# Sliding-window attention in two layers: the two key blocks of a query block folded into 128 columns

## What is computed

```python
WINDOW = BLOCK = 128
kb, vb = band(k), band(v)      # the previous block of 128 keys and the own one: 256 keys
s = einsum('bnqkgd,bnskd->bnkgqs', qb, kb) * HEAD_DIM ** -0.5
rel = qi + BLOCK - sj          # qi: query in its block, sj: key in the band
mask = (rel >= 0) & (rel < WINDOW) & (kpos >= 0)
s = where(mask, s, -inf)
m = maximum(max(s), sink)
p = exp(s - m)
p = p / (sum(p) + exp(sink - m))
o = einsum('bnkgqs,bnskd->bnqkgd', p, vb)
```

## Time and profile before

| | |
|---|---|
| median of 3 runs | 2209.37 us (2207.12 to 2209.56) |
| the profiled execution | 2209.6 us |
| its span, first to last instruction | 2207.7 us |
| TensorE busy | 2189.7 us (99%) |
| VectorE busy | 1191.6 us (54%) |
| ScalarE busy | 977.1 us (44%) |
| GpSimd busy | 1059.2 us (48%) |
| attention groups of layer 0 | about 129.8 to 279 us of the span |
| attention groups of layer 1 | 675.9 us later, the same pattern |

### The profile page before, as it was taken

The page is one execution under the profiler, slowest core; times in us unless marked ns, Lnnn a source line. Parts: engine busy times, 40 slices in busy tenths (PEclk is TensorE's granted clock), DMA queues, the critical chain, the costliest instruction groups (busy, mean ns, idle before and its releaser), DMA issues.

```text
span 2207.7 us, 29108 instructions
## 1 busy us (share of the span) xinstructions
PE 2189.7 (99%) x10471; PEld 1763.7 (80%) x10473; DVE 1191.6 (54%) x1536; ACT 977.1 (44%) x1549; POOL 1059.2 (48%) x525
## 2 busy tenths in 40 slices
PE   9999999999999999999999999999999999999999
PEld 7877778888888887778888888887787678888887
DVE  7877863222446877874222345858787745333301
ACT  5567633322214567744333214336645654444311
POOL 4963344444444883244444443433666653444442
PEclk9999999999999999999999999999999999999999
DMA  5332232333662332132333572321221012333332
GB/s 179 107 89 58 67 96 86 98 99 98 209 210 88 110 100 61 58 88 94 95 95 95 179 239 87 96 82 63 69 93 49 29 55 87 101 99 96 95 95 86
DMA packets 62870, 219.58 MB, mean 99 GB/s; under 512 B 7936, under 2 KB 8192, under 8 KB 62784
## 3 DMA queue, kind: packets, MB, share of 16 engines
q1 hardware_dynamic: 55296, 191.16, 29.0%
q10 hardware_dynamic: 7488, 27.27, 3.6%
HBM read 212.76 MB, written 2.10 MB: 97 GB/s over the span
## 4 chain that ended last, share of the span: by engine, by line
PE 92%; DVE 4%; ACT 2%; issue 1%; POOL 1%; DMA 0%; SPq 0%; ACTq 0%; POOLq 0%; DVEq 0%
PE bank L1691 28%; PE bank L1693 27%; PE bank L1692 27%; PE bank L1874 1%; PE bank L1946 1%; PE bank L1920 1%; PE bank L1765 1%; PE bank L2229 1%; ACT prob L650 1%; PE bank L2240 1%; POOL soft_lo L473 0%; DVE conv L1260 0%; PE bank L2273 0%; DVE conv L1262 0%; DMA raw<-stream 0%
## 5 line engine op out<-in xcount | busy, mean ns | idle before, releaser
L390 POOL TENSOR_TENSOR wl<-raw,wh 128x1024 fp32r<-128x1024 f32 x349 | 852.6, 2444 | 1029.9 <-ACT wh L529 1029.8
L1691 PE MATMUL bank<-hh,wh 128*128 128x512 f32 (+1 forms) x1984 | 775.2, 391 | 5.4 <-ACT root L866 2.1
L1693 PE MATMUL bank<-hh,wl 128*128 128x512 f32 (+1 forms) x1984 | 765.1, 386 | 0.0
L1692 PE MATMUL bank<-hl,wh 128*128 128x512 f32 (+1 forms) x1984 | 764.5, 385 | 0.0
L529 ACT ACTIVATE wh<-raw 128x1024 fp32r<-128x1024 f32 x351 | 369.7, 1054 | 586.5 <-PE bank L1693 543.9
L1691 PEld LDWEIGHTS bank<-hh,wh 128*128 128x128 f32 x1984 | 373.4, 188 | 90.4 <-issue 11.1
L1693 PEld LDWEIGHTS bank<-hh,wl 128*128 128x128 f32 x1984 | 373.4, 188 | 75.7
L1692 PEld LDWEIGHTS bank<-hl,wh 128*128 128x128 f32 x1984 | 373.7, 188 | 74.5 <-issue 1.7
L1691 PE MATMUL bank<-ah,wh 128*128 (+1 forms) x512 | 201.7, 394 | 0.0
L1693 PE MATMUL bank<-ah,wl 128*128 (+1 forms) x512 | 200.7, 392 | 0.0
L1692 PE MATMUL bank<-al,wh 128*128 (+1 forms) x512 | 198.7, 388 | 0.0
(11 more groups left out here) (374 smaller groups left out, 2786.0 us busy)
## 6 DMA issues: line engine op xcount, KB each, us to landing
raw<-stream SPq DMA_DIRECT2D x351, 512.0 KB, 3.6
ada_w<-ada ACTq DMA_DIRECT2D x48, 512.0 KB, 4.5
x<-x_t ACTq DMA_DIRECT2D x4, 512.0 KB, 7.7
out_t<-x SPq DMA_DIRECT2D x8, 256.0 KB, 2.1
th<-q SPq DMA_DIRECT2D x16, 64.0 KB
th<-q SPq DMA_DIRECT2D x64, 16.0 KB
q<-th SPq DMA_DIRECT2D x16, 64.0 KB, 2.0
cst<-consts SPq DMA_DIRECT2D x1, 640.0 KB, 5.7
```

The costliest lines, as they stand in the source:

```text
L390: nc.gpsimd.tensor_tensor(wl[:, slot, :], raw[:, raw_slot, :], wh[:, slot, :].bitcast(F32), ALU.subtract).then_inc(lo_ready, 1)
L1691: mm(dst, wh[:, slot, w], xh, start=start, stop=False)
L1692: mm(dst, wh[:, slot, w], xl, start=False, stop=False)
L1693: return mm(dst, wl[:, slot, w], xh, start=False, stop=stop)
```

## The change

Scores of a query block are no longer accumulated on a mask. TensorE writes both key blocks' scores to PSUM as they are. ScalarE copies the previous block's 128 columns (or, for n = 0, the mask) to `prob` in SBUF (`base`), VectorE overwrites those columns that belong to the own block (`copy_predicated`, with the constant `later`), and maximum, exponentials and normalisation then work on 128 columns in SBUF. TensorE makes four transposes for every group. ScalarE copies the transposed weights out once; VectorE multiplies them by the constant `keep`, which leaves those of the own block (`keep_own`). The value product uses the identity: all weights times V of the previous block, plus kept weights times (V own - V previous), the difference being made once a layer (`v_step`, in the memory of `v_t`). `prob_t` and the PSUM bank of the transposes become double. The mask matmuls, `put_mask` and the semaphore `masked` go; `base_ready` and `kept_out` are new. The diff, with unchanged lines and semaphore declarations cut:

```diff
--- before.py
+++ after.py
@@ -100,8 +100,8 @@
...
-            prob = sb("prob", [P, 2, 4, 2 * P], F32, region)
-            prob_t = sb("prob_t", [P, 2, 4, P], F32, region)
+            prob = sb("prob", [P, 2, 4, P], F32, region)
+            prob_t = sb("prob_t", [P, 2, 2, 4, P], F32, region)
...
@@ -313,6 +313,16 @@
...
+        def kept_before(l, g):
+            return 12 * l + g - (g + 3) // 4
+        def score_block(g, w):
+            b = 2 * (g % 2)
+            return bank[:, b:b + 2, :].rearrange("p a (c w d) -> p (a c) w d", c=2, w=2)[:, :, w, :]
+        turned_bank = lambda g: 5 - g % 2
+        v_step = v_t[:, :].rearrange("p (a b) -> p a b", a=BLK)
...
@@ -640,24 +650,20 @@
...
                 def exps(g):
...
-                    lo = P if n == 0 else 0
-                    b = 2 * (g % 2)
...
-                    if g >= 2:
-                        act.wait_ge(turned, 16 * l + g - 1)
...
-                        kv, at = i // 2, n * NH + 2 * (2 * j + i % 2) + i // 2
-                        af(prob[:, g % 2, i, lo:], bank[:, b + kv, (i % 2) * 2 * P + lo:(i % 2 + 1) * 2 * P], ACT.Exp,
+                        at = n * NH + 2 * (2 * j + i % 2) + i // 2
+                        af(prob[:, g % 2, i, :], prob[:, g % 2, i, :], ACT.Exp,
...
-                def put_mask(g):
-                    lo = P if group(g)[0] == 0 else 0
-                    b = 2 * (g % 2)
-                    act.wait_ge(exp_ready, 16 * l + g - 1)
-                    af(bank[:, b:b + 2, :].rearrange("p a (c d) -> p (a c) d", c=2)[:, :, lo:],
-                       win_mask[:, lo:2 * P].unsqueeze(1).to_broadcast([P, 4, 2 * P - lo]), ACT.Copy).then_inc(masked, 1)
+                def base(g):
+                    act.wait_ge(scores_ready, 16 * l + g + 1)
+                    if g >= 2:
+                        act.wait_ge(turned, 16 * l + g - 1)
+                    before = score_block(g, 0) if group(g)[0] else win_mask[:, P:2 * P].unsqueeze(1).to_broadcast([P, 4, P])
+                    af(prob[:, g % 2, :, :], before, ACT.Copy).then_inc(base_ready, 1)
...
@@ -667,17 +673,16 @@
...
+                base(0)
+                base(1)
                 exps(0)
...
-                put_mask(2)
...
                 def probs_out(g):
...
-                    if g >= 1:
-                        act.wait_ge(pv_ready, 16 * l + g)
-                    if group(g)[0] > 0:
-                        af(prob_t[:, 0, :, :], bank[:, 4, :].rearrange("p (a b) -> p a b", a=4), ACT.Copy)
-                    af(prob_t[:, 1, :, :], bank[:, 5, :].rearrange("p (a b) -> p a b", a=4), ACT.Copy).then_inc(turned_out, 1)
+                    if g >= 2:
+                        act.wait_ge(pv_ready, 16 * l + g - 1)
+                    af(prob_t[:, g % 2, 0, :, :], bank[:, turned_bank(g), :].rearrange("p (a b) -> p a b", a=4), ACT.Copy).then_inc(turned_out, 1)
...
@@ -687,17 +692,16 @@
...
                 for g in range(CO_FROM):
                     probs_out(g)
+                    if g + AHEAD < 16:
+                        base(g + AHEAD)
...
-                        put_mask(3)
...
                         exps(g + AHEAD)
-                    if g + 2 * AHEAD < 16:
-                        put_mask(g + 2 * AHEAD)
...
                     if g == LN_MEAN:
@@ -716,6 +720,7 @@
...
                 probs_out(13)
+                base(15)
                 exps(15)
...
@@ -1145,7 +1150,9 @@
...
                 dve.wait_ge(vt_turned, l + 1)
-                nc.vector.tensor_copy(v[:, :, :], bank[:, M_VT % 4, :].rearrange("p (a b) -> p a b", a=BLK)).then_inc(lin_free, 2)
+                v_bank = bank[:, M_VT % 4, :].rearrange("p (a b) -> p a b", a=BLK)
+                link(nc.vector.tensor_copy(v[:, :, :], v_bank))
+                tt(v_step[:, 1:BLK, :], v_bank[:, 1:BLK, :], v[:, 0:BLK - 1, :], ALU.subtract).then_inc(lin_free, 2)
                 invert(q_scale[:, :], q_root[:, :])
...
@@ -1153,11 +1160,13 @@
...
                 def maxima(g):
...
-                    lo, b, s = (P if n == 0 else 0), 2 * (g % 2), g % 2
+                    s = g % 2
...
-                    link(nc.vector.reduce_max(row_max[:, s, :], bank[:, b:b + 2, :].rearrange("p a (c d) -> p (a c) d", c=2)[:, :, lo:], AX.X))
+                    dve.wait_ge(base_ready, 16 * l + g + 1)
+                    link(nc.vector.copy_predicated(prob[:, s, :, :], minus_later.bitcast(I32).unsqueeze(1).to_broadcast([P, 4, P]), score_block(g, 1)))
+                    link(nc.vector.reduce_max(row_max[:, s, :], prob[:, s, :, :], AX.X))
...
@@ -1165,13 +1174,20 @@
...
                 def normalise(g):
-                    (n, j), s = group(g), g % 2
-                    lo = P if n == 0 else 0
+                    s = g % 2
...
-                    w = 2 * P - lo
-                    tt(prob[:, s, :, lo:], prob[:, s, :, lo:], rden[:, s, :].unsqueeze(2).to_broadcast([P, 4, w]), ALU.mult).then_inc(probs_ready, 1)
+                    tt(prob[:, s, :, :], prob[:, s, :, :], rden[:, s, :].unsqueeze(2).to_broadcast([P, 4, P]), ALU.mult).then_inc(probs_ready, 1)
+                def keep_own(g):
+                    if group(g)[0] == 0:
+                        return
+                    dve.wait_ge(turned_out, 16 * l + g + 1)
+                    if g >= 2:
+                        dve.wait_ge(pv_ready, 16 * l + g - 1)
+                    tt(prob_t[:, g % 2, 1, :, :], bank[:, turned_bank(g), :].rearrange("p (a b) -> p a b", a=4),
+                       keep.unsqueeze(1).to_broadcast([P, 4, P]), ALU.mult).then_inc(kept_out, 1)
...
@@ -1212,6 +1228,7 @@
...
                 for g in range(CO_FROM):
+                    keep_own(g)
                     if g == LN_MEAN:
...
@@ -1263,12 +1280,14 @@
...
+                keep_own(13)
                 maxima(15)
                 merge(0)
...
                 gate_conv(2, 6)
+                keep_own(14)
                 merged_rest(0)
...
@@ -1277,6 +1296,7 @@
...
                 gate_conv(4, 6)
+                keep_own(15)
                 merge(4)
...
@@ -1863,16 +1883,13 @@
                     if g == 1:
...
-                        pe.wait_ge(masked, 14 * l + g - 1)
-                    else:
-                        for kv in range(2):
-                            mm(bank[:, b + kv, :], ident_bf[:, :], win_mask[:, :], start=True, stop=False, skip_group_check=True)
+                        pe.wait_ge(max_ready, 2 * (16 * l + g - 1))
                     for i in range(2):
...
                         for kv in range(2):
                             half = slice(HD * kv, HD * kv + HD)
...
-                                      k[half, (n - 1) * P + lo:n * P + P], start=False, stop=True, skip_group_check=True)
+                                      k[half, (n - 1) * P + lo:n * P + P], start=i == 0, stop=True, skip_group_check=True)
                     last.then_inc(scores_ready, 1)
...
@@ -1911,13 +1928,13 @@
                     pe.wait_ge(probs_ready, 16 * l + g + 1)
...
-                    else:
-                        pe.wait_ge(turned_out, 16 * l + g)
                     if g == 1:
...
-                    for w in range(1 if n == 0 else 0, 2):
-                        for i in range(4):
-                            last = nc.tensor.transpose(bank[:, 4 + w, i * P:i * P + P], prob[:, g % 2, i, w * P:w * P + P], ident)
+                    if g >= 2:
+                        pe.wait_ge(turned_out, 16 * l + g - 1)
+                        pe.wait_ge(kept_out, kept_before(l, g - 1))
+                    for i in range(4):
+                        last = nc.tensor.transpose(bank[:, turned_bank(g), i * P:i * P + P], prob[:, g % 2, i, :], ident)
                     last.then_inc(turned, 1)
...
@@ -1940,11 +1957,16 @@
...
                         pe.wait_ge(pv_out, 16 * l + g)
-                    for w in range(1 if n == 0 else 0, 2):
+                    for kv in range(2):
+                        half = slice(HD * kv, HD * kv + HD)
+                        last = mm(bank[half, 7, 0:2 * P], v[:, max(n - 1, 0), half], prob_t[:, g % 2, 0, 2 * kv:2 * kv + 2, :].rearrange("p a b -> p (a b)"),
+                                  start=True, stop=n == 0)
+                    if n:
+                        pe.wait_ge(kept_out, kept_before(l, g + 1))
                         for kv in range(2):
                             half = slice(HD * kv, HD * kv + HD)
-                            last = mm(bank[half, 7, 0:2 * P], v[:, n - 1 + w, half], prob_t[:, w, 2 * kv:2 * kv + 2, :].rearrange("p a b -> p (a b)"),
-                                      start=w == (1 if n == 0 else 0), stop=w == 1)
+                            last = mm(bank[half, 7, 0:2 * P], v_step[:, n, half], prob_t[:, g % 2, 1, 2 * kv:2 * kv + 2, :].rearrange("p a b -> p (a b)"),
+                                      start=False, stop=True)
                     last.then_inc(pv_ready, 1)
...
@@ -2429,7 +2451,7 @@
...
-    put("later", -1.0 * (i[:, None] >= i[None, :]))
```

(5 more changed lines are left out.)

## The result

The changed kernel takes 2213.05 us (median of 16 runs, 2211.78 to 2213.87), the kernel before 2208.62 us beside it (16 runs, 2207.10 to 2209.59). The ratio is 1.0019, with a 95% interval of 1.0012 to 1.0026: it is slower by some 4 us. The profiled execution took 2213.81 us, its span is 2211.9 us.

What follows compares the result with a forecast made beforehand. TensorE, busy for 2189.7 of 2207.7 us, was taken to bound the kernel, with VectorE level in places. Per layer 5.76 - 0.79 - 1.45 - 2.28 = 1.24 us, 2.5 us for two, giving 2206.9 us; range 2200 to 2214.

Steps and rivals of the forecast that it cites:

- What leaves TensorE: Attention on TensorE: four fewer transposes in twelve groups (0.43 or 0.38 us each) and no mask matmuls; 5.76 us a layer.
- The masks' 0.75 us: Group 1's scores would start 0.75 us earlier without mask matmuls, limited by the wait for gate(1) on VectorE.
- Place 1: Groups 1 to 3, tile after gate(5): TensorE would arrive 2.04 us earlier, 1.25 kept, 0.79 us lost.
- Place 2: Group 6: variance step L1220 stands behind keep_own(6), which waits for ScalarE, so the next tile starts late; 1.45 us lost.
- `keep_own` is done by then: Value product: TensorE's new wait for kept_out stands behind a tile or half tile, so keep_own finishes first; no cost.
- Place 3: Groups 8 to 12: tile after gate(13) starts 1.21 us later instead of 1.29 earlier; 2.28 us lost.
- The tail of groups 13 to 15: Last groups, followed by half tiles: four fewer transposes save TensorE 0.38 us in each group.
- What was to show it: Sign for groups 8 to 12: weight load after gate(13) idle by about 2.6 us, released by L1144.
- at nothing: Groups 8 to 12: VectorE's saving in the iteration before, on layer norm products beside GpSimd's subtraction, counted as zero.
- The prices: New instruction times: predicated copy 0.69 us, keep_own 0.69 us on VectorE; ScalarE's exponentials 459 ns each in place of 561.
- the dear copy: Rival, chance 0.14: predicated copy takes 1.38 us by also reading the old destination; 6.9 us more, 2213.8 us.
- the chain comes along: Rival, chance 0.28: waits for GpSimd shrink, groups 1 to 3 and 8 to 12 cost nothing; 2200.3 us.

Runs made afterwards that it cites:

- all three edits: Changed kernel with v_step after q_minus, GpSimd's subtraction behind maxima(2), and the variance step ahead of keep_own(6): 2203.48 us, ratio 0.9975.
- the fastest version: Changed kernel with all three edits, plus GpSimd's subtractions held behind VectorE's layer norm products in iterations 8 to 10: 2198.1 us, ratio 0.9953.
- the same three waits: Kernel before, with GpSimd's subtractions of iterations 8 to 10 held behind VectorE's layer norm products: 2207.32 us, ratio 0.9997; on all three edits: 2198.1 us.

## Why the prediction was wrong, point by point

The prediction said 2206.9 us and no measurable difference; the time is 2213.05 us, within the range of 2200 to 2214, but slower by a measurable 0.19%. The range was right only by its width. In its own steps, for layer 0:

- **What leaves TensorE: right.** Four transposes take 0.52 to 0.59 us start to start in groups 0 to 12, and an undisturbed group is 0.43 us shorter: from one group's transposes to the next's 8.34 us (217.08 to 225.42) in place of 8.77 (215.08 to 223.85). Ahead of half tiles they take 0.35 to 0.41 us, which saves 0.44 a group, not the 0.38 taken.
- **The masks' 0.75 us and "`v_step` ... before `gate(1)`, where VectorE is idle for 1.62 us": this step failed.** The 0.5 us do lie in the idle time (L1155 took 0.56). But `q_minus` and the taps are queued behind `v_step`, and I didn't ask what GpSimd does at the time when `q_minus` now starts. `gate(1)` went from 129.88 to 130.85, and the scores of group 1 started 0.18 us later instead of 0.75 earlier, 0.93 us lost (1.12 with the 0.19 of the start). The kernel with `v_step` behind `q_minus` gives back 1.09 us a layer.
- **Place 1, 1.25 us kept of 2.04: this step failed.** It assumed that the chain of groups 1 to 3 changes by its own durations alone. The durations of VectorE's new instructions were about right, but the step left out that ScalarE's `base` stands ahead of the maximum (0.70 us in group 2, where no `keep_own` covers it), and it left out GpSimd: in group 2 the three small operations, at 0.16 us each, slid behind L400, L423 and L424. The kernel that holds GpSimd back gives back 2.0 us a layer. 1.09 + 2.0 = 3.1 us, which is what separates +1.85 from -1.25 (with the start, 3.1 of 3.3). With all three edits the tile after `gate(5)` starts at 163.83 in place of 164.88, 1.05 us earlier than in the kernel before, for the 1.25 forecast. So with the orders restored place 1 comes out nearly as forecast, though by luck in part, since `base` is in it now and wasn't counted.
- **Place 2, 1.45 us: right.** The tile is released by the variance, 1.38 us idle and 1.44 later than its own pace; the kernel with the variance first takes 1.37 us back.
- **"`keep_own` is done by then": this step failed too.** The sentence on TensorE's new wait for `kept_out` took it to cost nothing. The rows above show two stalls of exactly that kind, 0.58 us at 155.38 and 1.05 us at 234.71, each released by `keep_own` (L1189). Both have the same root as places 1 and 3, since VectorE reaches `keep_own` late there, and both are gone in the fastest version.
- **Place 3, 2.28 us: the sum held, the reason not.** From group 8 to the transposes of group 13 TensorE fell back by 1.34 us (3.33 - 1.99), against 1.21 - 0.22 = 0.99 forecast; the loss is 2.63 us, mis-sized by 0.35. The tail of groups 13 to 15 gave 1.31 us for the 1.14. What was to show it came otherwise: the weight load after `gate(13)` was to be idle for about 2.6 us and was for 0.65, and the loss is spread over TensorE's stalls of 0.57 after `gate(12)`, 1.05 in the value product of group 10, 0.25 at `gate(13)` and two smaller ones. And what was lost there was not VectorE's work: the sentence that counted the iteration before "at nothing", since its products stand beside GpSimd's subtraction, named the 4.1 us a layer that would have paid for all of it.
- **The prices.** The predicated copy takes 711 to 750 ns, for 690 taken, and doesn't wait for GpSimd (at 162.09, inside a GpSimd subtraction that runs from 160.78 to 163.19, it takes 0.74 us); `keep_own` 678 to 692 ns, as taken; the exponentials out of SBUF 485 ns, 26 more than taken, the very difference of L634 and L680. So the dear copy, the rival that ended on the slow side, fell. The time came out near its 2213.8 us by another cause. The view of one source line of the changed kernel for each, and the grouping by lines from 125 to 290 us:

```profile
L1168 DVE COPY_PREDICATED prob<-cst,bank x32: 711/732/750, 133.8 to 937.7; 128x512 f32<-128x512 int32 x32
...
L1189 DVE TENSOR_TENSOR prob_t<-bank,cst x24: 678/691/692, 154.6 to 953.1; 128x512 f32<-128x512 f32 x24
...
L1171 DVE TENSOR_TENSOR row_max<-row_max,q_minus x32: 161/164/2364, 135.3 to 939.2; 128x4 f32<-128x4 f32 x32
...
L656 ACT ACTIVATE prob<-prob,neg_max,q_scale 128x128 f32<-128x128 f32 x64 | 30.9, 485 | 43.7 <-DVE neg_max L1172 43.7
```

The third row shows how misleading a median is here: that of the small operation has fallen from 430 to 164 ns against the earlier trace rows, as the rival "the chain comes along" hoped. Its worst case has risen from 1991 to 2364 ns, and it is the one at 147.59 that counts.

The sum for layer 0: 3.26 us missed = 3.10 (masks and place 1) + 0.35 (place 3) - 0.17 (tail), with place 2 at nothing; two layers make 6.5 us. With the 0.19 us of the start it is 3.45 us a layer; the profiled execution is 6.7 us above the 2207.1 of the sum, which is two layers less the start. The prediction had the warning in hand, L1162 with 161 ns at best and 1991 at worst, and its rule of the Trainium skill (page "SBUF — State Buffer", section "Who interferes with whom") was put to the new instructions, which it clears, and to the layer norm's products, but not to the small operations and `q_minus`, whose start the change moves. The prediction also gave the rule without its exception: at most one SBUF input is harmless only outside the modes that use both ports. The same section says that a `tensor_scalar` within SBUF can take the shared ports as well, that whoever issues first has them for its whole instruction, and that the other is blocked. The trace agrees for `q_minus`, which has one input: it takes 0.20 us when it starts 0.61 us ahead of GpSimd, and 2.39 us when it starts 0.06 behind.

Two things stay open. Of the 3.5 us by the ratios that holding GpSimd back gives, the trace would have 4.0; the intervals are wider than that difference. And why the two last stalls (0.48 and 0.35 us at `gate(4)` and `gate(5)`) stay in the fastest version wasn't tried. Together they are 0.83 us, close to the 0.79 that place 1 put down; by the earlier trace rows the margin there was 0.46 us to begin with. The trace of that version names a candidate: from 149.11 us to `gate(4)` at 154.21 VectorE runs without a gap, and three of its instructions with two SBUF inputs take 0.51, 1.52 and 0.50 us there instead of 0.16, 0.69 and 0.16, beside GpSimd. No run holds GpSimd back at this place.

## What to carry to other kernels

When an edit delays VectorE, list for each instruction that it shifts what GpSimd starts within the shift, old and tiny instructions above all: hidden work isn't free if it changes who comes first. Where such a pair meets, hold back the engine that has slack (here GpSimd, by a wait of 0.65 us) rather than speed up the other. And time that is saved beside a bound engine shows only once that engine has become shorter: the same three waits gave nothing measurable on the old kernel and some 5 us on the new one.

## What the runs showed of the hardware that was not expected

- A VectorE instruction of 4 or 64 columns pays for a whole GpSimd instruction if it starts 0.05 us behind it: 0.16 to 2.36 us and 0.20 to 2.39 us. The two that follow, 4 columns each, take 1.21 us and end with the next two GpSimd instructions.
- A predicated copy of 128x512 from PSUM into SBUF, with its predicate in SBUF, takes 0.73 us, 0.04 more than a product of one operand in PSUM and one in SBUF, and all 32 lie between 711 and 750 ns, which leaves no room for a second pass of 0.68 us over the old destination.
- A stall of TensorE costs more than the idle time shown. Sets of matmuls follow each other before the end shown of the last one (0.48 us from start to start for a set of 0.65), and around a stall this overlap is lost. From L1962 to L1968 it is 0.48 us when nothing waits (199.80 to 200.28), and 1.23 us where L1968 is shown idle for 0.58: 0.75 us lost for 0.58 shown. The ten stalls of over 0.2 us in layer 0, with 7.3 us of idle time together, therefore should weigh more than that. The comparison of starts in the table above counts the loss.
